# The mixer of a two-layer block, reordered: projection units, convolution taps and recurrence interleaved, some taps computed by ScalarE and GpSimd, norms applied after the matmuls

## The chip, the cores and the metric

The kernel runs on one core of a Trainium2 chip. The metric is the device time of one launch in microseconds. TensorE (PE) multiplies matrices, VectorE (DVE), ScalarE (ACT) and GpSimd (POOL) work elementwise, and SyncE (SP) issues the weight loads.

## The reference, cut to what matters

512 tokens of width 1024 pass a block of a mixer and a retrieval feed-forward (`peer_ffn`), then two attention layers with feed-forwards. The change concerns the mixer and what is next to it:

```python
def hybrid_mixer(n, w_in, ...):                     # n = rms_norm(h, mix_norm_g)
    z = n @ w_in                                     # 1024 -> 2048
    x_lru, g_lru, a_glu, b_glu = split(z, 4)         # 512 channels each
    xc = depthwise_conv(x_lru, lru_conv_w, ...)      # 4 taps
    h_fwd, h_bwd = rg_lru(xc, ...), rg_lru(xc, ..., reverse=True)
    y_lru = (h_fwd + h_bwd) * gelu(g_lru)
    glu = a_glu * sigmoid(b_glu)
    c = depthwise_conv(glu, conf_conv_w, ...)        # 31 taps
    y_conv = silu(group_layer_norm(c))               # groups of 64 channels
    y = concat([rms_norm(y_lru, beta_lru), rms_norm(y_conv, beta_conv)])
    return y @ w_out                                 # then h = h + this

# rg_lru: a = exp(log_a), log_a = 8 * sigmoid(gate r) * log_sigmoid(lam)
#         u = sqrt(-expm1(2 * log_a)) * sigmoid(gate i) * xc, scanned along the tokens
# peer_ffn(rms_norm(h, ffn_norm_g)): queries, top 16 keys of each head, 16384-row tables
# gathered by index, softmax gates, a weighted sum of rows
```

## The kernel before

Every tensor of the mixer lies with 128 channels on the partitions and the 512 tokens along the free axis, so 512 channels are four tiles, called c = 0 to 3. The code is a queue of instructions for each engine, written out by hand, with semaphores between them. There is no planner: the order in each queue is the order of the text.

**Projection.** `w_in` comes in 16 units of 512 KB (eight 128x128 blocks each) through a ring of four buffers, which SP fills (L1562). `stream` (L384) runs eight matmuls for a unit into one of four PSUM banks and waits until the bank's former tile was drained (`tile_drained`). The units come in the order `pairs`: first the four pairs of a_glu and b_glu, then the four of x_lru, then the four of g_lru. Before the first unit the whole norm stands: ScalarE squares the eight tiles of x (L363), TensorE sums them with a matrix of ones (L372), ScalarE takes the root (L367), VectorE its reciprocal (L377) and eight scaled tiles (L380). At the start PE also forms the rows of position biases (L1586), which later attention layers use; ScalarE copies them (L1635) and stores them to DRAM.

**Convolution.** VectorE multiplies a_glu and sigmoid(b_glu) out of PSUM (L1753) and then does all 31 taps of tiles 0 and 1, and later of tiles 2 and 3, in `scalar_tensor_tensor` instructions of 128x512 with the accumulator as second input (L1757, L1762). The 4 taps on x_lru follow (L1773, L1778).

**Gates and recurrence.** TensorE forms four gates for each tile (L1601), ScalarE their sigmoids (L1665), then eight Tanh (L1672) and eight Exp (L1677). VectorE turns the tanh into 1 - a*a by a division over 128x2048 elements, twice (L1793 to L1798, the reciprocal is L1796), ScalarE takes the root (L1681), and VectorE scans both directions (L1806).

**Norms of the mixer and output.** Group means and variances come from matmuls with a block matrix (L1608, L1612); VectorE takes four reciprocals (L1814) and products (L1816), ScalarE the SiLU (L1693). Both halves are then normalised in full (L363 to L380 again, once for each) before `stream` starts the eight units of `w_out`. VectorE adds each tile to the residual h (L544), ScalarE squares it, and the norm of the feed-forward again stands as a whole before the first query matmul (L596).

**Retrieval.** `peer_pe`, `peer_act`, `peer_dve` and `peer_pool` run 256 groups of two rows: GpSimd gathers them (L888), VectorE takes dot products (L827), ScalarE a GELU (L726), VectorE makes two diagonal matrices (L838), TensorE adds the weighted rows (L639). The first lookup begins with the copy at L753. Buffers return to GpSimd through `uv_used`.

`Steps.do` counts VectorE's own instructions, and `settle` waits for all of them. An instruction that reads what the one before wrote waits in this way.

## Time and profile before

| | |
|---|---|
| median of 3 runs | 3395.56 us (3392.03 to 3396.84) |
| the profiled execution | 3395.28 us, its span 3393.5 us |
| mixer and norms, to the first query matmul | 0 to 372.0 us |
| first lookup on VectorE | 390.84 us |
| gathers and their sums | to 1761.6 us |
| attention layers and feed-forwards | 1761.6 to 3393.5 us |
| mean granted TensorE clock | 0.964 of full |

The span is the part of the execution that the trace covers, and the execution's own time is 1.8 us longer. Times in rows are microseconds from the start of the span unless marked ns. A row of a timeline gives the start, the duration, engine, line, operation, what it writes and reads, and the count if several equal ones were merged; in square brackets is the idle time before it and what ended it. In a row of the chain the work is only the part that set the end.

### The profile page before, as it was taken

Reading aid. Unit: us, or ns where it says so; the run is one execution under the profiler, and the core shown is the slowest. Engines: PE = TensorE matmul, PEld = TensorE weight load, DVE = VectorE, ACT = ScalarE, POOL = GpSimd, SP = SyncE. Lnnn points to the kernel's source line nnn. Section 1 sums busy time; section 2 is a strip of 40 time slices with the busy share of each in tenths; the row PEclk is TensorE's granted clock in tenths of the full one; section 3 lists DMA queues with packets and bytes.
Section 4 is the critical chain, followed back from the end, with each engine's and each line's share of the span. In section 5 each row is a group of like instructions: output and inputs, shape, how many; then the busy total and the mean of one; then the engine's idle time right before and its main releaser. Section 6 shows DMA issues by size and latency. Waiting matters only on the chain.

```text
span 3393.5 us, 33892 instructions
## 1 busy us (share of the span) xinstructions
PE 2881.5 (85%) x11216; PEld 1744.1 (51%) x11216; DVE 1953.8 (58%) x5012; ACT 786.5 (23%) x1550; POOL 1141.6 (34%) x804
## 2 busy tenths in 40 slices
PE   6846888977777777777779998999999989999998
PEld 2312434423332222232238865688788867568876
DVE  2964366678888888888763486444212147344411
ACT  2041111111111111111121286222132147422211
POOL 0000023354444444444433232244444433134442
PEclk9877999999999999999999999999999999999999
DMA  3101389999999999999972111222222222122221
GB/s 95 58 17 43 136 306 353 345 410 427 427 427 427 426 427 427 426 417 425 419 289 75 51 51 49 79 95 93 95 85 93 92 75 80 34 82 97 94 94 67
DMA packets 121784, 696.21 MB, mean 205 GB/s; under 512 B 15003, under 2 KB 19243, under 8 KB 55435
## 3 DMA queue, kind: packets, MB, share of 16 engines
q0 software_dynamic: 74352, 543.06, 38.8%
q1 hardware_dynamic: 47184, 150.88, 13.8%
q10 hardware_dynamic: 124, 0.75, 0.1%
q8 instruction: 62, 1.02, 0.1%
q14 instruction: 62, 0.51, 0.0%
HBM read 692.30 MB, written 2.34 MB: 205 GB/s over the span
## 4 chain that ended last, share of the span: by engine, by line
PE 58%; DMA 23%; DVE 8%; issue 4%; ACT 3%; POOL 2%; DVEq 0%; SPq 0%; ACTq 0%; POOLq 0%
PE ps L520 30%; DMA arena<-in_peer_uv,arena 16%; PE ps L397 8%; PE ps L639 7%; DMA n<-in_peer_uv,arena 4%; DMA ring<-in_peer_uv,arena 3%; PE ps L596 3%; PE ps L1086 2%; PE ps L1102 2%; PE ps L1073 2%; POOL arena L888 2%; DVE arena L827 1%; ACT arena L1124 1%; PE ps L372 1%; PE ps L1347 1%
## 5 line engine op out<-in xcount | busy, mean ns | idle before, releaser
L639 PE MATMUL ps<-arena 128*128 128x512 f32 x1560 | 741.8, 621 | 215.0 <-DVE arena L838 214.7
L417 POOL TENSOR_TENSOR w_lo<-ring,w_hi 128x1024 fp32r<-128x1024 f32 (+1 forms) x176 | 459.2, 2609 | 745.9 <-ACT w_hi L430 745.9
L888 POOL DMA_INDIRECT arena<-in_peer_uv,arena x390 | 419.9, 1077 | 715.9 <-PE ps L639 544.0
L639 PEld LDWEIGHTS ps<-arena 128*128 128x128 f32 x1560 | 292.4, 196 | 655.2 <-DVE arena L838 342.2
L827 DVE CUSTOM_DVE_ANT_0 arena<-arena,sq 128x1024 f32<-128x1024 f32 x390 | 462.7, 1224 | 215.2 <-DMA arena<-in_peer_uv,arena 213.8
L520 PE MATMUL ps<-n_hi,w_hi 128*128 128x512 f32 x1152 | 461.7, 401 | 6.2 <-ACT n_hi L457 5.8
L520 PE MATMUL ps<-n_lo,w_hi 128*128 128x512 f32 x1152 | 455.9, 400 | 4.2 <-DVE n_lo L462 4.0
L520 PE MATMUL ps<-n_hi,w_lo 128*128 128x512 f32 x1152 | 457.1, 397 | 0.0
L430 ACT CAST w_hi<-ring 128x1024 fp32r<-128x1024 f32 (+1 forms) x176 | 194.8, 1107 | 770.9 <-PE ps L520 769.7
L726 ACT ACTIVATE arena<-arena 128x2 f32<-128x2 f32 x256 | 52.1, 203 | 1134.6 <-DVE arena L827 1134.6
L520 PEld LDWEIGHTS ps<-n_lo,w_hi 128*128 128x128 f32 x1152 | 219.0, 190 | 61.5 <-DVE n_lo L462 9.3
L520 PEld LDWEIGHTS ps<-n_hi,w_hi 128*128 128x128 f32 x1152 | 219.2, 190 | 60.0 <-issue 9.0
L544 DVE TENSOR_TENSOR h<-ps,h 128x512 f32<-128x512 f32 x40 | 27.7, 692 | 383.8 <-PE ps L520 222.5
L520 PEld LDWEIGHTS ps<-n_hi,w_lo 128*128 128x128 f32 x1152 | 218.6, 190 | 52.1 <-issue 0.5
L397 PE MATMUL ps<-n,ring 128*128 128x512 f32 x384 | 172.6, 613 | 33.8 <-DVE n L380 18.1
L838 DVE TENSOR_SCALAR arena<-consts,arena,tcmp 128x128 f32<-128x128 f32 x512 | 153.5, 342 | 0.0
L945 DVE TENSOR_TENSOR arena<-ps,rstd 128x512 f32<-128x512 f32 x44 | 30.5, 692 | 207.2 <-PE ps L520 207.2
L520 PE MATMUL ps<-hid_hi,w_hi 128*128 128x512 f32 x352 | 138.7, 394 | 12.4 <-DVE hid_lo L954 12.4
L639 PE MATMUL ps<-ring,arena 128*128 128x512 f32 x240 | 112.7, 613 | 38.6 <-DVE arena L838 38.6
L639 PE MATMUL ps<-n,arena 128*128 128x512 f32 x248 | 114.3, 603 | 34.9 <-DVE arena L838 34.9
L397 PEld LDWEIGHTS ps<-n,ring 128*128 128x128 f32 x384 | 75.5, 198 | 131.0 <-issue 120.6
L520 PE MATMUL ps<-hid_lo,w_hi 128*128 128x512 f32 x352 | 138.4, 393 | 0.0
(245 smaller groups left out, 3904.9 us busy)
## 6 DMA issues: line engine op xcount, KB each, us to landing
ring<-in_a_up SPq DMA_DIRECT2D x44, 512.0 KB, 3.7
ring<-in_b_up SPq DMA_DIRECT2D x44, 512.0 KB, 3.7
ring<-in_b_q SPq DMA_DIRECT2D x24, 512.0 KB, 3.7
ring<-in_a_down SPq DMA_DIRECT2D x16, 704.0 KB, 4.0
ring<-in_b_down SPq DMA_DIRECT2D x16, 704.0 KB, 4.0
ring<-in_a_in SPq DMA_DIRECT2D x20, 512.0 KB, 3.7
ring<-in_w_in SPq DMA_DIRECT2D x16, 512.0 KB, 3.7
ring<-in_w_q SPq DMA_DIRECT2D x16, 512.0 KB, 5.7
```

The source lines that it names most:

```text
L397: mm = pe.matmul(bank(j), ring[:, j, k * P:(k + 1) * P], rhs[k], start=k == 0, stop=k == kt - 1)
L417: pool.tensor_tensor(w_lo[:, j % 2, 0:kt * P], ring[:, j, 0:kt * P], w_hi[:, j % 2, 0:kt * P], ALU.subtract).then_inc(split_lo, 1)
L430: act.copy(w_hi[:, j % 2, 0:kt * P], ring[:, j, 0:kt * P]).then_inc(split_hi, 1)
L520: mm = pe.matmul(bank(j // 2 if two else j), w[:, j % 2, cols], r[:, x, :], start=no == 0 and not (two and j % 2), stop=no == len(passes) ...
L596: mm = pe.matmul(bank(2 + x), ring[:, u % RING, k * P:(k + 1) * P], ns[k], start=k == 0, stop=k == DK - 1)
L639: mm = pe.matmul(bank(2 * (tt % 2) + q), diag[:, no % DIAGS, r, :], uvrow[p][r][:, D + 512 * q:D + 512 * q + 512], start=slot + r == 0, st ...
L827: ins = dve.tensor_tensor_reduce(out=u, in0=u, in1=ntok[:, tt, :], scale=1.0, scalar=0.0, op0=ALU.mult, op1=ALU.add, accum_out=dots[:, p, ...
L838: ins = dve.tensor_scalar(diag[:, no % DIAGS, r, :], ident, gel[:, p, r:r + 1], gate[:, tt, slot + r:slot + r + 1], ALU.mult, ALU.mult)
L888: pool.indirect_dma_start(uvrow[p][r], None, t["peer_uv"], bass.IndirectOffsetOnAxis(ap=expert_id[:, tt, slot + r:slot + r + 1], axis=0)). ...
L1073: pe.matmul(b.scores, b.q, b.keys, start=True, stop=True).then_inc(L.scores_ready, 1)
L1086: tr = pe.transpose(ps[0:width, 4 + no % 2, P * x:P * x + P], L.p[:, s % 3, at:at + width], ident)
L1102: mm = pe.matmul(ps[64 * half:64 * half + 64, out_bank(L, it), P * qt:P * qt + P], v, L.pt[0:width, s % 2, P * x:P * x + P], start=y == 0, ...
```

## The change

The parts, in the order of the launch:

1. **Loads.** x comes in four pieces with a semaphore each, the first unit of w_in after the first piece; vec is loaded by ScalarE's queue; the constants come after the second unit. The one-hot table and the bias rows leave the start: SP loads the table in two halves when all lookups are done, TensorE forms one row chunk behind each of eight late groups (`BIAS_AT`), ScalarE copies it and stores the rows in two DMAs.
2. **Norm of the mixer late.** ns is x times the gain only (a `tensor_scalar`). TensorE starts on unit 0 as pieces of x arrive; the squares are added on VectorE and one matmul sums them. Each drained unit is multiplied by rstd (`drain`, VectorE, from PSUM). Before, ScalarE or the GLU product read the bank itself.
3. **Order.** Units go b_glu, a_glu for tiles 0 and 1, then x_lru, then tiles 2 and 3, then g_lru. PE's queue puts group means, variances and gates between units, VectorE's queue puts drains and norms between taps.
4. **Taps split.** Of 31 taps of a tile, the first 15, 15, 12 and 8 (`POOL_TAPS`) are products on ScalarE into four buffers (`PRODS`), added by GpSimd in two alternating sums. VectorE does the other 16, 16, 19 and 23 into two partial sums, adds them, and adds GpSimd's sum (`conv_merge`).
5. **Recurrence.** 1 - a*a comes from a square and one `scalar_tensor_tensor` (`lru_weight`); the two 2048-wide reciprocals with their `tensor_scalar` are gone. GpSimd multiplies igate and xc (128x2048, twice).
6. **Group norm.** A matrix I - mean centres a tile in one matmul; the four subtractions on VectorE are gone.
7. **Norms of the output late.** w_out multiplies y_conv * beta_conv and y_lru * beta_lru * ratio, where ratio is the quotient of both norms' factors. The factor of y_conv is applied to each finished tile before the residual. Units 0 to 3 take their convolution half first.
8. **Norm of the feed-forward late.** Queries and dot products use h times the gain; the factor for each token is given to Exp and Gelu as their scale (`tok_scale`).

The queues of the mixer after, cut to the order and the new functions:

```diff
+POOL_TAPS = (15, 15, 12, 8)
+PRODS = 4
...
+        LOOKUPS_DONE = ALL_GROUPS - 2 * GROUPS
+        BIAS_AT = [ALL_GROUPS - x for x in (13, 12, 11, 10, 7, 6, 5, 4)]
...
+                act.activation(ex, ex, ACT.Exp, scale=tok_scale[:, tt:tt + 1]).then_inc(ex_done, 1)
...
@@ sync
+                    sp.wait_ge(ids_ready, TT * PH)
+                    sp.dma_start(relb[0:NBUCKET, :], t["rel_bias_2"]).then_inc(rel_in, 16)
+                    for x in range(2):
+                        if x:
+                            sp.wait_ge(row_ready, 4)
...
+                    load_x(0)
+                    load(0, 0, True)
+                    for k in range(1, TT):
+                        load_x(k)
+                    load(0, 1, True)
+                    sp.dma_start(consts[:, :], t["consts"]).then_inc(const_in, 16)
+                    load(0, 2, True)
+                    load(0, 3, True)
@@ tensor
-            norm_mean(pe, "mix", ones_d)
-            pe.wait_ge(n_ready, norm_tiles["mix"] + DK)
-            stream(pe, "w_in", ns)
...
+            project(0)
+            pe.wait_ge(const_in, 16)
+            pe.wait_ge(row_added, DK - 1)
+            pe.matmul(bank(4), ones_d, sq[:, 0, :], start=True, stop=True).then_inc(mean_done, 1)
+            for u in range(1, 7):
+                project(u)
+            pe.wait_ge(root_done, MEANS["mix"])
+            center_group(0)
+            project(7)
+            group_variance(0)
+            project(8)
+            center_group(1)
+            project(9)
+            group_variance(1)
+            project(10)
+            project(11)
+            lru_gates()
+            center_group(2)
+            project(12)
+            group_variance(2)
+            center_group(3)
+            project(13)
+            group_variance(3)
+            project(14)
+            project(15)
...
+            for j in range(RING):
+                out_unit(j, range(LK, DK))
...
+            for j in range(RING):
+                out_unit(j, range(LK))
+            for j in range(RING, DK):
+                out_unit(j, [*range(LK, DK), *range(LK)])
@@ scalar
+            def products(c, taps):
+                act.wait_ge(glu_ready, c + 1)
+                for tap in taps:
+                    x = first_prod[c] + tap
+                    if x >= PRODS:
+                        act.wait_ge(pool_added, prod_used[x - PRODS])
+                    act.activation(prods[:, x % PRODS, :], gpad[:, c, tap:tap + T], ACT.Copy,
+                                   scale=col("conf_w", LK * tap + c)).then_inc(prod_ready, 1)
...
+            sigmoid(0)
+            products(0, range(9))
+            sigmoid(1)
+            products(0, range(9, POOL_TAPS[0]))
+            products(1, range(10))
+            center_square(0)
+            products(1, range(10, POOL_TAPS[1]))
+            group_root(0)
+            sigmoid(2)
+            conv_out(0)
+            center_square(1)
+            group_root(1)
+            products(2, range(6))
+            sigmoid(3)
+            products(2, range(6, 9))
+            keep_gates(0)
+            products(2, range(9, 11))
+            keep_gates(1)
+            products(2, range(11, POOL_TAPS[2]))
+            products(3, range(2))
+            keep_gates(2)
+            products(3, range(2, 4))
+            keep_gates(3)
+            products(3, range(4, POOL_TAPS[3]))
...
@@ vector
+            def conv_taps(c, between={}):
...
+                    if i >= 2:
+                        dve.wait_ge(dve_step, marks[i - 2])
+                        step.do(dve.scalar_tensor_tensor(out=x, in0=src, scalar=w, in1=x, op0=ALU.mult, op1=ALU.add))
...
+            conv_taps(0)
+            drain(2, sigb[:, 1, :])
+            drain(3, glu_in(1))
+            glu(1, 3)
+            conv_taps(1, {8: lambda: drain_x(0)})
+            conv_merge(0)
+            lru_conv(0)
+            for c in range(1, LK):
+                drain_x(c)
+                lru_conv(c)
+            conv_merge(1)
+            normalize(0)
+            drain(8, sigb[:, 2, :])
+            drain(9, glu_in(2))
+            glu(2, 9)
+            conv_taps(2, {3: lambda: normalize(1), 10: lambda: drain(10, sigb[:, 3, :])})
+            drain(11, glu_in(3))
+            glu(3, 11)
+            conv_taps(3, {8: lambda: conv_merge(2)})
+            conv_merge(3)
+            drain(12, gelug[:, 0, :])
+            lru_weight(0)
+            lru_weight(1)
+            drain(13, gelug[:, 1, :])
+            normalize(2)
+            lru_scan(0)
+            normalize(3)
+            drain(14, gelug[:, 2, :])
+            lru_scan(1)
+            drain(15, gelug[:, 3, :])
...
@@ gpsimd
+            for c in range(LK):
+                conv_adds(c)
+            pool.wait_ge(gates_read, 4 * LK)
+            for d in range(2):
+                pool.tensor_tensor(igate[:, d], igate[:, d], xc, ALU.mult).then_inc(ix_ready, 1)
```

`conv_adds` is `POOL_TAPS[c] - 1` instructions `tensor_tensor` of 128x512 with both inputs in SBUF: 14, 14, 11 and 7. `normalize` is a reciprocal (128x512) and a product; `lru_scan` a product (128x2048) and four scans; `lru_conv` one `tensor_scalar` and three dependent `scalar_tensor_tensor`; `conv_out` on ScalarE a SiLU, a square and a copy. ScalarE's queue goes on with the eight Tanh, `center_square(2)`, four Exp and a square for each direction, `center_square(3)`, the roots, three GELUs, `conv_out` of tiles 1 to 3 and the last GELU, then the root of the convolution's norm and the squares of y_lru.

## Rows read from the trace of the kernel before

**Rows 1.** The page: the span, and busy time of each engine.

```profile
span 3393.5 us, 33892 instructions
...
PE 2881.5 (85%) x11216; PEld 1744.1 (51%) x11216; DVE 1953.8 (58%) x5012; ACT 786.5 (23%) x1550; POOL 1141.6 (34%) x804
```

**Rows 2.** The chain that ended last, 0 to 400 us: start us, us, what.

```profile
1.19 15.12 DMA h<-in_x
...
123.46 58.01 PE ps L397 x128
...
208.40 12.97 DVE arena L1796
...
297.60 57.98 PE ps L397 x128
...
372.04 15.43 PE ps L596 x32
```

**Rows 3.** Busy time of each engine in the mixer's recurrence.

```profile
186.00:300.00 114.00, 30.49 (x57) 12.37 (x56) 86.11 (x42) 40.63 (x56) 0.55 (x1) 0.65 0.01 2
```

**Rows 4.** First microseconds: the last two columns are DMA share and GB/s.

```profile
4.00:8.00 4.00, 0.00 (x0) 0.00 (x0) 0.00 (x0) 0.00 (x0) 1.93 (x3) 1.00 0.96 292
...
12.00:16.00 4.00, 0.07 (x1) 0.00 (x0) 0.00 (x0) 0.00 (x0) 0.00 (x0) 1.00 0.99 185
```

**Rows 5.** Timeline of VectorE in the mixer, then the first lookup.

```profile
124.88 39.87 DVE L1762 SCALAR_TENSOR_TENSOR arena<-arena,vec 128x512 f32<-128x512 f32 x60
...
244.57 4.57 DVE L1806 TENSOR_TENSOR_SCAN arena<-arena 128x512 f32<-128x512 f32 x4
...
260.50 3.35 DVE L1814 RECIPROCAL arena<-sq 128x512 f32<-128x512 f32 x1
263.88 0.69 DVE L1816 TENSOR_TENSOR arena<-arena 128x512 f32<-128x512 f32 x1
...
355.62 0.69 DVE L544 TENSOR_TENSOR h<-ps,h 128x512 f32<-128x512 f32 x1 [6.17 <-PE ps L397]
...
390.84 0.29 DVE L753 COPY arena<-arena 128x256 f32<-128x256 f32 x1 [18.85 <-ACT arena L709]
```

**Rows 6.** Timeline of ScalarE in the mixer.

```profile
201.06 1.28 ACT L1677 ACT_TABLE_LOAD   x1
202.35 5.01 ACT L1677 ACTIVATE arena<-arena 128x512 f32<-128x512 f32 x8
...
244.18 2.17 ACT L1687 ACTIVATE sq<-arena 128x512 f32<-128x512 f32 x4
```

**Rows 7.** Timeline of TensorE: eight instructions, then eight like them.

```profile
278.05 6.01 PE L372 MATMUL ps<-sq,consts 128*128 128x512 f32 x8 [27.60 <-ACT sq L363]
285.35 3.70 PE L372 MATMUL ps<-sq,consts 128*128 128x512 f32 x8 [1.30 <-ACT sq L363]
```

**Rows 8.** GpSimd's groups by shape, whole span: count, busy, mean ns.

```profile
L417 POOL TENSOR_TENSOR w_lo<-ring,w_hi 128x1024 fp32r<-128x1024 f32 x144 | 355.8, 2471 | 598.9 <-ACT w_hi L430 598.9
L417 POOL TENSOR_TENSOR w_lo<-ring,w_hi 128x1408 fp32r<-128x1408 f32 x32 | 103.3, 3229 | 147.0 <-ACT w_hi L430 147.0
...
L1257 POOL TENSOR_SCALAR arena<-arena 128x512 f32<-128x512 f32 x8 | 15.9, 1992 | 46.8 <-DVE arena L1167 46.8
```

**Rows 9.** Timeline of GpSimd, 1766 to 1775 us.

```profile
1766.73 2.35 POOL L417 TENSOR_TENSOR w_lo<-ring,w_hi 128x1024 fp32r<-128x1024 f32 x1 [1.64 <-ACT w_hi L430]
1771.96 2.56 POOL L417 TENSOR_TENSOR w_lo<-ring,w_hi 128x1024 fp32r<-128x1024 f32 x1 [2.87 <-ACT w_hi L430]
```

**Rows 10.** Timeline of VectorE at the same time.

```profile
1767.30 2.33 DVE L462 SCALAR_TENSOR_TENSOR n_lo<-h,in_gain,n_hi 128x512 fp32r<-128x512 f32 x1 [2.17 <-ACT n_hi L457]
...
1772.21 2.86 DVE L462 SCALAR_TENSOR_TENSOR n_lo<-h,in_gain,n_hi 128x512 fp32r<-128x512 f32 x1
```

**Rows 11.** Busy time of each engine in the gather stage.

```profile
1000.00:1400.00 400.00, 301.82 (x651) 118.20 (x650) 331.01 (x974) 45.05 (x112) 172.91 (x161) 0.99 1.01 427
```

**Rows 12.** The chain late in the gather stage.

```profile
1730.53 20.89 DMA n<-in_peer_uv,arena
```

More of the change, by code:

```diff
@@ L284, in program @@
         assert max(a.at, a2.at) <= ARENA - 4 * 11 * P
+        assert after <= 14000
+        relb = Region(14000).take(NH)
+        tail = Region(28 * T)
+        onehot, rowbuf = tail.take(HALF_ROWS), tail.take(HALF_ROWS)
         tabA = Region(ARENA - 4 * 11 * P).take(2, 2, 896)
@@ L621, in turn_tokens, with token_means @@
                     tr.then_inc(tok_turned, 1)
+            def token_means():
+                pe.wait_ge(row_added, 2 * DK - 2)
+                for tt in range(TT):
+                    mm = pe.matmul(ps[:, 1, tt:tt + 1], sq[:, 0, P * tt:P * tt + P], ones_d[:, 0:1], start=True, stop=True)
+                mm.then_inc(mean_done, 1)
             for hd in range(HEADS_FIRST):
@@ L1613, in _, with project @@
-            pe.wait_ge(cstd_ready, LK)
-            norm_mean(pe, "conv", ones_l)
-            norm_mean(pe, "lru", ones_l)
-            pe.wait_ge(n_ready, norm_tiles["lru"] + LK)
-            stream(pe, "w_out", ns)
+            def project(u):
+                if u >= RING:
+                    wait_tile(pe, u)
+                pe.wait_ge(w_landed[u % RING], 16 * (u // RING + 1))
+                for k in range(DK):
+                    if u == 0:
+                        pe.wait_ge(mix_ready, k + 1)
+                    mm = pe.matmul(bank(u % RING), ring[:, u % RING, k * P:(k + 1) * P], ns[k], start=k == 0, stop=k == DK - 1)
+                mm.then_inc(unit_done, 1)
@@ L1658, in _ @@
-            for c in range(LK):
+            act.dma_start(vec[:, :], t["vec"]).then_inc(vec_in, 16)
+            for k in range(DK):
+                act.wait_ge(x_in[k // 2], 16)
+                act.activation(sq[:, k, :], hs[k], ACT.Square).then_inc(row_squared, 1)
+            act.wait_ge(lam_dve, 1)
+            act.activation(lamw[:, 1, :], lamw[:, 0, :], ACT.Exp, scale=-1.0).then_inc(lam_act, 1)
+            act.wait_ge(const_in, 16)
+            act.wait_ge(mean_done, MEANS["mix"])
+            act.activation(std[:, :], bank(4), ACT.Sqrt, bias=eps).then_inc(root_done, 1)
@@ new lines, in _ @@
+            for k in range(1, DK):
+                dve.wait_ge(row_squared, k + 1)
+                if k >= 2:
+                    dve.wait_ge(row_added, k - 1)
+                dve.tensor_tensor(sq[:, 0, :], sq[:, 0, :], sq[:, k, :], ALU.add).then_inc(row_added, 1)
+            dve.wait_ge(lam_act, 1)
+            dve.tensor_scalar(lamw[:, 2, :], lamw[:, 1, :], 1.0, None, ALU.add).then_inc(lam_dve, 1)
+            dve.wait_ge(root_done, MEANS["mix"])
+            step.do(dve.reciprocal(rstd[:, :], std[:, :]))
@@ new lines, in conv_merge, with lru_conv @@
+            def conv_merge(c):
+                dve.wait_ge(pool_added, pool_ops[c + 1])
+                step.settle()
+                dve.tensor_tensor(cacc[:, c, :], cacc[:, c, :], parts[:, 2 * (c % 2), :], ALU.add).then_inc(conv_ready, 1)
+            def lru_conv(c):
+                dve.wait_ge(tile_drained, 4 + c + 1)
+                step.do(dve.tensor_scalar(xc[:, c, :], xpad[:, c, 0:T], col("lru_w", c), col("lru_b", c), ALU.mult, ALU.add))
+                for tap in range(1, LRU_TAPS):
+                    step.settle()
+                    ins = dve.scalar_tensor_tensor(out=xc[:, c, :], in0=xpad[:, c, tap:tap + T], scalar=col("lru_w", LK * tap + c),
+                                                   in1=xc[:, c, :], op0=ALU.mult, op1=ALU.add)
+                    if tap < LRU_TAPS - 1:
+                        step.do(ins)
+                    else:
+                        ins.then_inc(xc_ready, 1)
@@ new lines, in lru_scan @@
+            def lru_scan(d):
+                dve.wait_ge(root_ready, d + 1)
+                dve.wait_ge(ix_ready, d + 1)
+                step.do(dve.tensor_tensor(igate[:, d], igate[:, d], wrk[:, d], ALU.mult))
+                step.settle()
+                for c in range(LK):
+                    order = slice(None, None, -1) if d else slice(None)
+                    step.do(dve.tensor_tensor_scan(tanh_la[:, d, c, order], rgate[:, d, c, order],
+                                                   igate[:, d, c, order], 0.0, ALU.mult, ALU.add))
@@ L1800, in _ @@
[L1800 to L1807 removed]
+                                     op0=ALU.mult, op1=ALU.add).then_inc(lam_dve, 1)
```

482 lines of the change are left out of this document (286 added, 196 removed).

## The prediction, made before the changed kernel had run

> **What bounds the kernel now.** I read the page first: TensorE is busy for 85% of the span and VectorE for 58% [rows 1], but these are means over stages, and the change touches only what stands before the first query matmul at 372.04 us. So the chain comes next [rows 2]. It runs through the arrival of x (to 16.31 us), the projection (58 us for eight units behind the first convolution), the recurrence with VectorE's reciprocals of 12.97 us, then 57.98 us for w_out, and only then the queries. No two of these overlap on the chain. The windows confirm it: from 186 to 300 us VectorE is busy 86 of 114 us, TensorE 30, at 0.65 of its clock, and the DMA share is 0.01 [rows 3]. Behind the mixer stands the gather stage, whose DMA share is 1.01 at 427 GB/s [rows 11]; its bytes don't change, so a lookup that starts earlier should carry the whole rest of the launch along. The end to watch is therefore the first lookup at 390.84 us [rows 5].
>
> **Unit costs.** VectorE: a tap 39.87 / 60 = 0.665 us, a drain or product 0.69, a dependent one 0.72, a reciprocal 3.35, a scan 4.57 / 4 = 1.14 [rows 5]. ScalarE: 2.17 / 4 = 0.54 for a product, 1.28 for a table switch [rows 6]. TensorE: the tiles of w_out are 6.17 + 0.69 = 6.86 us apart [rows 5], and eight matmul instructions after an idle stretch took 6.01 us where the next eight took 3.70 [rows 7]: a cold start costs about 1.8 us for a unit.
>
> **The unknown: GpSimd's adds beside VectorE's taps.** Before, GpSimd does no 128x512 add. Its 128x1408 subtraction takes 3.229 us and its fastest 128x1024 one 2.35 [rows 8, 9]; the line through them gives 1.18 us for 512 columns, the line through the means (2.471) gives 1.46. I take 1.3. Below stands 1.18; above, its `tensor_scalar` of 128x512 at 1.99 [rows 8]. What an add does to VectorE is seen where both ran. GpSimd worked from 1766.73 to 1769.08; VectorE's instruction of 1767.30 took 2.33 us, to 1769.63, which is 0.55 after GpSimd's end. GpSimd worked from 1771.96 to 1774.52; the one of 1772.21 took 2.86, to 1775.07, again 0.55 behind [rows 9, 10]. Both have two inputs in SBUF, and so do taps and adds. VectorE doesn't slow down, it stands still. The GpSimd instruction also took 2.56 instead of 2.35, so it had waited for the one on VectorE, and then got in ahead of the next. I therefore let the two alternate and charge VectorE 1.25 us for each add, 4.6 for each 128x2048 product (twice the 2.35 of 1024 columns, less the part that overlaps).
>
> The Trainium skill says the same and sharper (SBUF — State Buffer, Who interferes with whom): a VectorE instruction with two SBUF inputs and a GpSimd one that reads SBUF exclude each other for a whole instruction, so work given to GpSimd is not taken off VectorE. By that rule the 46 adds cost 46 x 1.25 = 57 us of VectorE's time to save 50 taps, 33 us; this case's trace agrees at the two places above.
>
> **The walk through the new order.** I follow VectorE's queue and stop it only where a semaphore does.
> - *Norm.* The early DMA rate is 185 to 292 GB/s [rows 4]. x, the first unit, vec and gw are about 3.3 MB where before x, the table and gw were 3.1, so x ends near 15.5 us (range 13 to 17). Two scalings 1.1, seven dependent adds 5.0: 21.6. One cold matmul 1.7, root 0.7, reciprocal 3.35: rstd at 27.4. The norm is no longer ahead of unit 0, but it is ahead of the first drain.
> - *Tile 0.* Unit 1 ends at 23.3 + 6.9 + 1.8 = 32.0; drain, GLU and the small lambda operations: 35.1. Sixteen taps and a sum 17 x 0.665 = 11.3, fourteen adds 17.5: 63.9.
> - *Tile 1.* Two drains and GLU 2.1: 66.0. 11.3 + 0.7 + eight adds 10.0: 88.0. Only eight, since ScalarE's queue holds products 10 to 14 behind `center_square(0)`, which needs `conv_merge(0)`, which stands behind these taps. PE stands at `center_group(0)` from about 71 us too, so units 7 and later are late. Merge: 88.7.
> - *Four `lru_conv`* at 0.5 + 3 x 0.72 = 2.7: 10.8, three drains 2.1, the six adds left 7.5, `conv_merge(1)` 0.7: 109.8.
> - PE now gets `center_group(1)` 0.9 and unit 9, 6.9: 117.6; drain and GLU: 119.0.
> - *Tile 2.* Three taps, then a wait for group 1's deviation to about 122.4, `normalize` 4.1, the other seventeen instructions 11.3, a drain 0.7, five adds that hit them 6.3: 144.8. Drain and GLU: 146.2.
> - *Tile 3.* Twenty-five instructions 16.6, eleven adds (four of tile 2 are left) 13.8, both 2048-wide products 9.2: `conv_merge(3)` at 185.8.
> - *Recurrence.* PE can only now do `center_group(3)` and unit 13, cold: 9.5, to 195.3, and `drain(13)` waits for it in front of everything else. The two `lru_weight` (4.6) hide in that wait. Then drain 0.7, `normalize` 4.1, scan 2.3 + 4.6 = 6.9, `normalize` 4.1, drain 0.7, scan 6.9, drain 0.7: 219.4. Sums and products of four tiles 5.0: 224.4. The reciprocals of 2 x 12.97 us are gone.
> - *Output.* Square, add, matmul, root, reciprocal 3.35, ratio, first product: 7.9, to 232.3. PE meanwhile ends the convolution halves at 233.8. Four halves 13.7 and four units 27.5: 275.0, where before it was 355.6.
> - *Query.* The tiles of the last w_out unit need 2 us, covered by seven matmuls of the first query. Unit 0 ends at 281.9. Before, the lookup came 18.8 us after the query's start [rows 2, 5] with a cold start in it; now about 17.4. Lookup at 292.4.
>
> The gain is 390.8 - 292.4 = 98.4 us. Against it stand the table and the bias rows, 0.73 MB in a stage that moves 427 GB/s [rows 11]: 1.7 us. The matmul of a bias row fits: a group lasts 400 / (651 / 8) = 4.9 us, of which PE works 3.7 [rows 11], and one more costs 0.9. Sum: 3395.3 - 98.4 + 1.7 = 3298.6 against the profiled execution, 0.3 us from the median. I say 3299.
>
> ScalarE switches tables more often in the new order, four times on the stretch that ends at w_out, at 1.28 us by the row; the switch at 201.06 was followed at 202.35 by work [rows 6]. The Trainium skill (ScalarE: Activation LUTs, What ACT_TABLE_LOAD costs) counts 2.66 us with a drain for each; by it the time would be 5.5 us more, 3304, and the row speaks against it.
>
> **The rivals.**
> - *GpSimd and VectorE don't get in each other's way.* Then `conv_merge(3)` is set by PE's units and VectorE's own taps: 48.5 after tile 1's GLU, 78 after `conv_merge(1)` (unit 7), 90.8 at tile 2's GLU, 127.7 at the merge, 58 us earlier: 3241. Against it stand both stalls of [rows 9, 10]; for it, only that those were 1024 wide with a rounded output.
> - *An add is as long as the `tensor_scalar`*, 1.99 us [rows 8]: 0.74 more for 46 + 8 equivalents (a 2048-wide product is four): +40, 3339. For it, GpSimd's waits on semaphores between short adds; against it, the line through its own two-input shapes.
> - *The late table stalls the groups.* Its second half is asked for three groups (14.7 us) before its use; a transfer there took 20.89 us [rows 12]: 6.2 us for the wait, 3305. If all eight rows waited so, each for a copy behind a GELU, 50 us: 3349.
> - *Slower than before.* Gain and charge cross where an add holds VectorE for 1.25 + 96.7 / 54 = 3.0 us; then the taps alone eat the recurrence's saving. Only the 1408-wide instruction takes that long [rows 8], so this needs a handover of more than an add's own length each time.
>
> **The numbers.** Forecast (3285 to 3318 with its own uncertainties: x by 2 us, handovers of 0.05 to 0.2 us at 57 places, cold starts) 0.66; longer adds 0.15; no blocking 0.10; stalls at the late rows or another wait in the handwritten order 0.06; slower 0.03. The range 3250 to 3340 takes in the longer adds and most of the way to the free ones. 0.2% is 6.8 us, about what a measurement here can tell from no change: faster 0.96, same 0.01, slower 0.03.
>
> **What would show it.** In the changed profile: GpSimd's adds above 1.3 us each, near 1.8 where taps run; VectorE's taps alternating between 0.7 and 1.8 to 2.0; PE idle in front of the centring matmul from about 71 to 89 us and near 170 to 186; the lookup near 292; the gather stage as long as before. The prediction is wrong if taps keep 0.665 us beside adds, if `conv_merge(3)` is later than 200 us, or if the end of the gathers moves by less than the lookup.

## The result, and the profile after

Before: 3396.1 us (3392.03 to 3396.84, 4 runs). After: 3296.97 us (3292.27 to 3298.73, 4 runs). The ratio is 0.9708, 95% interval 0.9692 to 0.9725. The profiled execution took 3298.73 us. The forecast was 3299.0.

The page of the kernel after, span and busy times, as [rows 1]:

```profile
span 3296.9 us, 33551 instructions
...
PE 2856.2 (87%) x11182; PEld 1737.2 (53%) x11182; DVE 1960.2 (59%) x4995; ACT 858.7 (26%) x1614; POOL 1241.1 (38%) x855
```

The span is 96.6 us shorter, although VectorE is shown busy for 6 us more and GpSimd for 100 us more. Part of that busy time is one of them standing still for the other, as the experiments show. The gain comes from work laid side by side and from the reciprocals that are gone. The chain of waits, as [rows 2], shows where:

```profile
2.87 11.43 DMA h<-in_x
...
34.94 15.37 DVE arena L1942 x14
...
103.96 1.28 ACT L1801
105.25 0.82 ACT arena L1801
...
144.18 23.55 DVE arena L1942 x15
169.30 2.08 PE ps L1687 x2
171.37 8.13 PE ps L1680 x16
...
213.65 48.07 PE ps L1738 x112
...
268.58 0.79 PE ps L653 x8
```

Neither reciprocal of 12.97 us is left in it. Of the projection, which had a stretch of 58.01 us there, one unit is left (8.13 us). Of w_out's 57.98 us 48.07 are left (L1738): its 112 matmul instructions are seven units' worth, at sixteen a unit, so only one unit's worth was done early. VectorE's taps (L1942) are what the mixer now waits for until 169 us.

VectorE's timeline at the places that the walk named, as [rows 5]:

```profile
50.33 0.69 DVE L1949 TENSOR_TENSOR arena<-arena 128x512 f32<-128x512 f32 x1
...
168.55 0.69 DVE L1954 TENSOR_TENSOR arena<-arena 128x512 f32<-128x512 f32 x1
169.16 0.68 DVE L1922 TENSOR_TENSOR arena<-ps,rstd 128x512 f32<-128x512 f32 x1
169.76 4.48 DVE L1976 SCALAR_TENSOR_TENSOR arena<-arena 128x2048 f32<-128x2048 f32 x2
179.53 0.69 DVE L1922 TENSOR_TENSOR arena<-ps,rstd 128x512 f32<-128x512 f32 x1 [5.28 <-PE ps L1680]
...
279.72 0.29 DVE L830 COPY arena<-arena 128x256 f32<-128x256 f32 x1 [9.85 <-ACT arena L767]
```

The first lookup moved from 390.84 to 279.72 us, by 111.1, where I had expected 98.4. The total moved by less. So the first thing to see is that something gave 12.7 us more than forecast and something later took it back. Three lines of three views say where. They are 400 us of the gather stage, beginning 609 us after the first lookup as those of [rows 11] do (the last column is GB/s), SyncE's timeline where it starts the weights of the next layer, and the groups of TensorE's matmuls for the bias rows:

```profile
889.00:1289.00 400.00, 297.22 (x641) 116.29 (x640) 326.60 (x961) 53.03 (x111) 170.56 (x158) 0.99 1.01 421
```

```profile
1671.19 116.93 SPq L1650 DMA_DIRECT2D ring<-in_a_in  x20
```

```profile
L696 PE MATMUL ps<-arena x16: 345/589/600, 1610.0 to 1657.6; 33*16 33x512 f32 x14, 33*16 33x219 f32 x2
```

That first load waits for the last gathered row to be used, so it marks the end of the gather stage. Before, it stood at:

```profile
1761.86 39.87 SPq L1562 DMA_DIRECT2D ring<-in_a_in  x8
```

From the first lookup to it are 1371.0 us before and 1391.5 after. The DMA share is 1.01 in both, but 421 GB/s flow where 427 did. The rest of the span is 1631.6 us before and 1625.7 after. Together: -111.1 + 20.4 - 5.9 = -96.6. I had put 1.7 us where 20.4 stand.

The experiments use the same three pieces. I call them the mixer (to the first lookup), the gather stage (to the first `a_in` load) and the later layers (to the end of the span).

### The profile page after: what moved, and what is told of

Its sections match the earlier page's. It is cut to its first block, busy times and chain, and to the rows that moved or that the text cites. A ratio compares the mean times of both kernels' runs of the same rounds, so it can differ in the third digit from the quotient of the medians.

```text
span 3296.9 us, 33551 instructions
## 1 busy us (share of the span) xinstructions
PE 2856.2 (87%) x11182; PEld 1737.2 (53%) x11182; DVE 1960.2 (59%) x4995; ACT 858.7 (26%) x1614; POOL 1241.1 (38%) x855
## 4 chain that ended last, share of the span: by engine, by line
PE 54%; DMA 25%; DVE 10%; issue 4%; ACT 3%; POOL 2%; SPq 0%; DVEq 0%; ACTq 0%; POOLq 0%
PE ps L535 31%; DMA arena<-in_peer_uv,arena 16%; PE ps L674 7%; DMA ring<-in_peer_uv,arena 5%; DMA n<-in_peer_uv,arena 4%; PE ps L412 3%; PE ps L623 3%; DVE arena L1942 3%; PE ps L1166 2%; PE ps L1182 2%; PE ps L1153 2%; PE ps L1738 1%; POOL arena L968 1%; DVE arena L904 1%; ACT arena L1204 1%
## 5 line engine op out<-in xcount | busy, mean ns | idle before, releaser
L432 POOL TENSOR_TENSOR w_lo<-ring,w_hi 128x1024 fp32r<-128x1024 f32 (+1 forms) x176 | 465.9, 2647 | 733.8 <-ACT w_hi L445 733.8
L787 ACT ACTIVATE arena<-arena,tok_scale 128x2 f32<-128x2 f32 x256 | 75.5, 295 | 1093.1 <-DVE arena L904 1092.3
L535 PE MATMUL ps<-hid_hi,w_lo 128*128 128x512 f32 x352 | 138.6, 394 | 0.0
L1166 PE MATMUL ps<-consts,arena 128*128 128x128 f32 (+1 forms) x800 | 114.6, 282 | 23.5 <-ACT arena L1204 18.4
```

The costliest lines, as they stand in the source:

```text
L432: pool.tensor_tensor(w_lo[:, j % 2, 0:kt * P], ring[:, j, 0:kt * P], w_hi[:, j % 2, 0:kt * P], ALU.subtract).then_inc(split_lo, 1)
L535: mm = pe.matmul(bank(j // 2 if two else j), w[:, j % 2, cols], r[:, x, :], start=no == 0 and not (two and j % 2), stop=no == len(passes) ...
L787: act.activation(gel[:, p, :], dots[:, p, :], ACT.Gelu_apprx_tanh, scale=tok_scale[:, tt:tt + 1]).then_inc(gel_ready, 1)
L1166: tr = pe.transpose(ps[0:width, 4 + no % 2, P * x:P * x + P], L.p[:, s % 3, at:at + width], ident)
```

## The experiments

Two questions were open: what takes the 20 us in the gather stage, and whether GpSimd's adds cost or save. Nothing of the gathers is in the diff. But `center` adds 128 columns to `consts`, and `tok_std` and `tok_scale` are new. These stand ahead of the arena in SBUF. Added up from the allocations, the arena begins at byte 99840 before, a multiple of 256, and at 100416 after, 64 bytes past one. `n`, `sq` and the ring begin 128 bytes past a multiple of 256 in both kernels. Gathered rows of 8 KB land in the arena, `n` and the ring.

**A gap of 192 bytes ahead of the arena.**

```diff
+        sb("gap", [P, 48])
         arena_at = nc.sbuf_base
```

> The changed kernel with 192 bytes of padding in front of the arena, so that the gather buffers in it begin at a multiple of 256 bytes again (100608), as they did before the change (99840), where the change had moved them to 100416. The new constants and token factors (576 bytes) had done that. In the changed kernel the saturated gather stage moves 421 GB/s instead of 427 and its median packet takes 312 ns instead of 309, so 350 MB of gathers take 11.7 us more and the whole stage 20 us more. If the start address is the cause: 427 GB/s and 309 ns again, 12 to 16 us faster than the changed kernel, about 3283 us. Rival, the rate differs from chip to chip or run to run, or the longer ScalarE instructions with a scale set it: 421 GB/s here too and 3297 us.

Measured: 3287.3 us (3285.01 to 3288.99), ratio 0.9678 [0.9665, 0.9692]. The gather stage at its old rate, and its end:

```profile
889.00:1289.00 400.00, 301.83 (x650) 118.31 (x650) 330.87 (x976) 53.34 (x112) 168.39 (x161) 0.99 1.01 427
```

```profile
1655.80 118.28 SPq L1651 DMA_DIRECT2D ring<-in_a_in  x20
```

Mixer 278.7, gather stage 1377.1 (14.4 shorter), later layers 1631.0 (5.3 longer, as before the change). The rate is back at 427 GB/s, as the theory had it, but the total fell by 9.7 us and not by 12 to 16, because the later layers gave 5.3 back. The address of the arena sets the rate of the gathers. That it also sets something in the later layers I had not expected.

A stage as a whole is a coarse measure: in the kernel after and in the four kernels below that share its addresses it takes 1386.7 to 1391.5 us. Counted in the trace's packets of 8 KB, the stretch from the 24,000th to the 60,000th is finer. It takes 693.7 to 696.0 us in the five kernels of this document with the arena on a multiple of 256, and 704.6 to 707.0 in the six with it 64 bytes past.

**A second gap, so that n, sq and the ring begin at multiples of 256 bytes too.**

```diff
+        sb("gap0", [P, 32])
         h = sb("h", [P, DK, T])
...
+        sb("gap", [P, 16])
         arena_at = nc.sbuf_base
```

> As the one before, and 128 bytes of padding in front of h as well, so that the two gather buffers in n and the two in the weight ring, which start 128 bytes off a multiple of 256 in every kernel so far, are aligned too. If a start off the boundary costs about 1.4 to 2% of a packet: 2 of 7 buffer pairs gain it, 0.5% of 1170 us, another 4 to 7 us, about 3278 us, and more than 427 GB/s. Rival: no difference to the run before.

Measured: 3268.27 us (3265.55 to 3271.28), ratio 0.9624 [0.9611, 0.9637].

```profile
889.00:1289.00 400.00, 302.39 (x652) 118.36 (x650) 331.84 (x975) 53.33 (x112) 171.20 (x161) 0.99 1.01 427
```

The rate stays at 427 GB/s, where I had expected more: for a transfer, a start 128 bytes past costs nothing that shows here. The gather stage is 4.6 us shorter, but this is no gain of the rate: the whole of it lies ahead of the 16,000th packet, where kernels with the same addresses differ by as much (399.4 to 404.2 us from the first lookup to there in the five with the arena of the kernel after). The total is 19.0 us lower, and most of that came in the later layers, 1612.5 us in place of 1631.0, where TensorE is the bound.

**The kernel before, with its arena 64 bytes later.**

```diff
+        sb("gap", [P, 16])
         arena_at = nc.sbuf_base
```

> The kernel before with 64 bytes of padding in front of the arena and nothing else, so its gather buffers lose their 256-byte alignment (99904). If the start address is the cause: 421 GB/s in the saturated stage, packets of 312 ns, and 12 to 16 us slower than the kernel before, about 3410 us. Rival: 427 GB/s and 3396 us.

Measured: 3398.47 us (3394.94 to 3402.53), ratio 1.0007 [0.9998, 1.0016]. The total did not move, against the expectation. The pieces did:

```profile
1000.00:1400.00 400.00, 298.40 (x640) 116.95 (x639) 327.04 (x962) 44.83 (x111) 171.31 (x159) 0.98 1.01 421
```

```profile
1777.05 16.31 SPq L1563 DMA_DIRECT2D ring<-in_a_in  x5
```

Gather stage 1385.6 us (14.6 longer, as expected), later layers 1621.9 (9.7 shorter). Two effects of one address cancel. A total alone would have cleared the address of all blame.

**The kernel before, with n, sq, ring and arena all at multiples of 256 bytes.** This takes the second effect alone.

```diff
+        sb("gap0", [P, 32])
         h = sb("h", [P, DK, T])
...
+        sb("gap", [P, 32])
         arena_at = nc.sbuf_base
```

> The kernel before with two gaps in SBUF and nothing else: 128 bytes ahead of the first tensor, so that n, sq and the weight ring start at multiples of 256 bytes, and 128 bytes ahead of the arena, which stays at such a multiple. Theory (TensorE's products run a little faster when both operands start so: 232.1 to 227.3 ns per split matmul was seen between the kernels of the first batch): gather stage unchanged at 1371 us (+-3), the layers behind it 1610 to 1618 us in place of 1631.6, total 3374 to 3383. Rival (the shorter later layers of the all-aligned kernel came from elsewhere, or the arena's own place is what counts): total within 4 us of 3396.

Measured: 3376.18 us (3374.5 to 3376.95), ratio 0.9942 [0.9928, 0.9955]. Gather stage 1369.6, later layers 1613.0, all three as the theory had them. So two gaps and no other edit give 0.6%. Windows of 220 us, beginning about 420 us after the first `a_in` load (417 in the third), show it in TensorE's count. The first column behind the width is its busy time with the number of matmuls; the lines are of the kernel before, the kernel after, and this one:

```profile
2181.90:2401.90 220.00, 220.00 (x948) 178.35 (x947) 101.45 (x98) 51.72 (x60) 100.13 (x40) 1.00 0.31 97
```

```profile
2091.20:2311.20 220.00, 220.00 (x963) 180.51 (x962) 104.29 (x100) 52.88 (x60) 100.72 (x41) 1.00 0.29 98
```

```profile
2179.10:2399.10 220.00, 220.00 (x972) 182.23 (x971) 103.32 (x100) 53.06 (x60) 100.79 (x41) 1.00 0.30 100
```

TensorE is busy without a gap in all three, at the full granted clock, with 948, 963 and 972 matmuls: 232.1, 228.5 and 226.3 ns for one.

The same is seen over a whole up-projection of a feed-forward, by how long SyncE takes to issue its 44 weight loads, since each waits for a buffer that TensorE has used. The lines are of the first feed-forward before, of both in the kernel after, and of the first in this one:

```profile
2136.74 251.05 SPq L1562 DMA_DIRECT2D ring<-in_a_up  x44
```

```profile
2043.68 248.33 SPq L1650 DMA_DIRECT2D ring<-in_a_up  x44
...
2870.82 251.95 SPq L1650 DMA_DIRECT2D ring<-in_b_up  x44
```

```profile
2134.02 245.19 SPq L1564 DMA_DIRECT2D ring<-in_a_up  x44
```

In all kernels of this document it is 250.9 to 252.1 us with the arena on a multiple and the rest 128 bytes past (four stretches) and 245.2 to 246.3 with all on multiples (six). With the arena 64 bytes past it is 247.4 to 248.4 in ten stretches and 252.0 and 252.6 in two, the second one of the kernel after and the first one of the kernel with the old recurrence weight. So this address doesn't fix the pace alone, and why two stretches fell back isn't known. The trace also narrows down which products it concerns. In the up-projection one operand lies in `n` or `sq` (`n_hi`, `n_lo`) and the other in the arena (`w_hi`, `w_lo`). In the down-projection both lie in the arena (`hid_hi`, `hid_lo`), and SyncE's 16 loads for it take 114.4 to 116.3 us in all kernels, with no order by address.

**All taps on VectorE.** ScalarE's products and GpSimd's adds go, and `conv_merge` with them.

```diff
-POOL_TAPS = (15, 15, 12, 8)
+POOL_TAPS = (0, 0, 0, 0)
...
-            conv_taps(3, {8: lambda: conv_merge(2)})
-            conv_merge(3)
+            conv_taps(3)
...
-            for c in range(LK):
-                conv_adds(c)
```

> The changed kernel with the split of the taps undone: all 31 taps of a tile on VectorE in two partial sums, summed at once, no products on ScalarE and no adds on GpSimd; the order of the units and everything else stay. If VectorE stands still while GpSimd adds: VectorE's own 50 extra taps cost 50 x 0.665 = 33 us and the 46 adds, at about 1.0 us of standstill each in the changed kernel's trace, give back 46, and the centring of tiles 0 and 1 no longer waits for a late merge. The last centring then comes near 158 us instead of 169, the lookup about 11 us earlier, 3286 us. Rival, the split takes work off VectorE as it was meant to: the last centring comes 20 to 33 us later, 3317 to 3330 us.

Measured: 3281.25 us (3275.84 to 3281.59), ratio 0.9654 [0.9641, 0.9667], so faster than the kernel after. VectorE does 50 taps more and comes to the first lookup 11.6 us earlier, where the first theory had 11 and its rival had it come later. Its timeline with GpSimd idle (the first line) and beside GpSimd's two products of 2048 columns (the second), GpSimd's line, and the lookup:

```profile
33.99 19.30 DVE L1926 SCALAR_TENSOR_TENSOR arena<-arena,vec 128x512 f32<-128x512 f32 x29
...
129.39 27.86 DVE L1926 SCALAR_TENSOR_TENSOR arena<-arena,vec 128x512 f32<-128x512 f32 x29
...
268.15 0.29 DVE L827 COPY arena<-arena 128x256 f32<-128x256 f32 x1 [9.84 <-ACT arena L764]
```

```profile
131.50 9.96 POOL L2074 TENSOR_TENSOR arena<-arena 128x2048 f32<-128x2048 f32 x2 [125.46 <-ACT arena L1809]
```

The same 29 instructions take 8.56 us more beside GpSimd, nearly all of GpSimd's 9.96.

**The adds alone left out.** The products stay on ScalarE, the 74 taps on VectorE.

```diff
-                        act.wait_ge(pool_added, prod_used[x - PRODS])
+                        act.wait_ge(prod_ready, x - PRODS + 1)
...
-            for c in range(LK):
-                conv_adds(c)
```

> The kernel after, with GpSimd's 50 accumulating instructions left out: ScalarE still computes its 50 tap products and VectorE its 74 taps, but the products are never added, so the convolution misses those taps (and VectorE's sum is taken twice where the merge stood). Theory (GpSimd's adds hold up VectorE's taps): the taps fall to the 0.665 us each that the kernel with all taps on VectorE showed (29 in 19.30 us), so that 50 taps fewer than there take 50 x 0.665 = 33 us off its end of the taps (158.0), plus 4 merges of 0.7: the last merge ends at about 128 us, at most 135 if projection units are then late (169.2 in the kernel after); the first lookup comes at 240 to 248 us and the total is 3255 to 3272. Rival (the taps take as long without the adds, and something else spaces them): last merge at about 169, total within 5 us of the kernel after.

Measured: 3259.21 us (3254.07 to 3262.49), ratio 0.9597 [0.9584, 0.961]; first lookup at 243.71, last merge ending at 134.0. The first theory holds in all three. VectorE's first tile, against 15.44 us for the same 14 in the kernel after, and its last merge:

```profile
34.19 9.36 DVE L1942 SCALAR_TENSOR_TENSOR arena<-arena,vec 128x512 f32<-128x512 f32 x14
...
114.08 10.02 DVE L1942 SCALAR_TENSOR_TENSOR arena<-arena,vec 128x512 f32<-128x512 f32 x15
124.13 4.90 DVE L1949 TENSOR_TENSOR arena<-arena 128x512 f32<-128x512 f32 x1
129.06 4.90 DVE L1953 TENSOR_TENSOR arena<-arena 128x512 f32<-128x512 f32 x1
```

```profile
118.18 15.23 POOL L2097 TENSOR_TENSOR arena<-arena 128x2048 f32<-128x2048 f32 x2 [112.36 <-ACT arena L1812]
```

Two additions of 512 columns, 0.69 us elsewhere, took 4.90 each: one product of 2048 columns on GpSimd for each. And the lock works both ways. GpSimd's first product is shown from 118.18 on, yet the nine of the fifteen taps that were left went through at their own 0.67 us until 124.1. Its two took 15.23 us here, 9.96 above. Why it had to wait longer here than there stays open.

**The old recurrence weight in the new order.** Per direction a `tensor_scalar`, a reciprocal of 2048 columns and a product, in place of ScalarE's square and one product.

```diff
-                dve.scalar_tensor_tensor(out=wrk[:, d], in0=wrk[:, d], scalar=1.0, in1=tanh_la[:, d],
-                                         op0=ALU.add, op1=ALU.mult).then_inc(w_ready, 1)
+                step.do(dve.tensor_scalar(wrk[:, d], tanh_la[:, d], -1.0, 1.0, ALU.mult, ALU.add))
+                step.do(dve.reciprocal(wrk[:, d], wrk[:, d]))
+                dve.scalar_tensor_tensor(out=wrk[:, d], in0=tanh_la[:, d], scalar=-2.0, in1=wrk[:, d],
+                                         op0=ALU.mult, op1=ALU.mult).then_inc(w_ready, 1)
```

> The kernel after, with the recurrence's input weight computed the old way: per direction one VectorE tensor_scalar, the 2048-wide reciprocal and the product, in place of ScalarE's square and one product. From the rows before, per direction 1.22 + 12.95 us more on VectorE. Theory (both reciprocals lay on the path): from 169.8 us on, two times 16.5 us until 202.8, where the kernel after starts the drain of unit 13 at 179.5 because it waits 5.3 us for TensorE there: +23.3 us at that point, first lookup at 303, total 3315 to 3325. Rival (ScalarE and GpSimd are what the part waits for, the reciprocals fit into their waits): first lookup within 5 us of 279.7, total below 3303.

Measured: 3318.43 us (3311.81 to 3321.51), ratio 0.9772 [0.9758, 0.9785]; first lookup at 304.39. From 171.33 us on:

```profile
172.58 12.95 DVE L1972 RECIPROCAL arena<-arena 128x2048 f32<-128x2048 f32 x1
...
189.03 12.95 DVE L1972 RECIPROCAL arena<-arena 128x2048 f32<-128x2048 f32 x1
202.01 2.29 DVE L1974 SCALAR_TENSOR_TENSOR arena<-arena 128x2048 f32<-128x2048 f32 x1
204.22 0.68 DVE L1916 TENSOR_TENSOR arena<-ps,rstd 128x512 f32<-128x512 f32 x1
```

The drain of unit 13 comes 24.7 us later than in the kernel after and no longer waits, and the lookup is later by the same 24.7. These are the 28.4 us by which VectorE's instructions are longer, less the 5.3 us of wait for unit 13 that they fill, and 1.6 us by which the last merge had already ended later. The first theory holds, and the cheaper formula is worth 21.5 us in the median time, a good fifth of the whole gain.

**The bias rows in the mixer.** The table is loaded behind the first four weight units, and the eight matmuls stand behind projection unit 6, where TensorE would idle for 15.7 us.

```diff
                     load(0, 3, True)
+                    sp.dma_start(onehot[0:NBUCKET + 1, :], t["onehot"]).then_inc(onehot_in, 16)
+                    sp.dma_start(relb[0:NBUCKET, :], t["rel_bias_2"]).then_inc(rel_in, 16)
...
-                if no in BIAS_AT:
-                    bias_row(BIAS_AT.index(no))
```

> The kernel after, with the bias rows computed in the mixer again: table loaded behind the first four weight units, 8 TensorE products after projection unit 6, 8 ScalarE copies after the tenth product of tap tile 1, one store. Nothing of them is left in the gather stage, neither the table's transfer nor the 8 products in the last 13 groups. Theory (the late rows take about 6 of the 20 us that the gather stage lost): from the first lookup to the end of the gathers 1385.5 us against 1391.5, the mixer up to 1 us longer, total 3290 to 3294. Rival (the lost time is the transfers' slower pace alone): stage and total within 2 us of the kernel after. Second rival: the table's 0.5 MB among the first weight units holds the projection up by its 2.6 us and more, total unchanged.

Measured: 3287.24 us (3284.35 to 3288.38), ratio 0.9678 [0.9665, 0.9691]. First lookup at 279.09, next weights at:

```profile
1667.03 116.59 SPq L1609 DMA_DIRECT2D ring<-in_a_in  x20
```

The gather stage is 1387.9 us, 3.5 shorter, where 6 had been expected. By itself that is within the spread: with the late rows and the same addresses the kernel with the old recurrence weight needed 1386.7. The end of the stage decides it. From the 60,000th packet to the first `a_in` load the four kernels with late rows and these addresses take 126.2 to 127.3 us, and the two without (this one and the kernel before with its arena shifted) 123.5 and 123.3. So the rows cost about 3 to 4 us. The mixer doesn't take longer for it (both theories of a cost there fall), since TensorE and ScalarE had room before `center_group(0)`. The total gained 9.7 us, more than this explains. In the profiled executions 6.2 lie in the later layers, which the edit does not touch. 4.2 of those are in the second feed-forward. From its first weights to the load of the next matrix the kernel after needs 257.2 us in its profile, while three kernels with the same addresses as it (this one and the two above) need 252.8 to 253.0. This is the slow second up-projection of the kernel after (251.95 us). The kernel with the old recurrence weight has such a one in its first feed-forward (252.59). I count 3.5 us as shown and the rest as variation between executions.

**Together.** All taps on VectorE, all starts at multiples of 256 bytes, the rows early, and three edits in the order:

```diff
-            conv_taps(2, {3: lambda: normalize(1), 10: lambda: drain(10, sigb[:, 3, :])})
+            conv_taps(2, {18: lambda: normalize(1), 10: lambda: drain(10, sigb[:, 3, :])})
...
-                pool.tensor_tensor(igate[:, d], igate[:, d], xc, ALU.mult).then_inc(ix_ready, 1)
+                dve.tensor_tensor(igate[:, d], igate[:, d], xc, ALU.mult).then_inc(ix_ready, 1)
...
-            center_group(2)
-            project(12)
+            project(12)
+            project(13)
+            center_group(2)
```

> The version that the experiments point to: all 31 taps of each tile on VectorE, SBUF starts of n, sq, ring and arena at multiples of 256 bytes, bias rows computed in the mixer, normalize(1) after the 18th tap of tile 2 in place of the third, projection units 12 and 13 ahead of the third centring on TensorE, and the two 2048-wide products of the recurrence's input on VectorE in place of GpSimd. Sum from the runs: 3281.3 (all taps on VectorE), less 28.7 (all aligned, 3297.0 to 3268.3), less 3.5 to 5 for the rows, less 4.5 and 5.0 us of VectorE's waits for the second group root and for unit 13, less 3.7 (two products of 2.28 us on VectorE in place of the 8.3 us by which GpSimd's held VectorE up): about 3235, within 3225 to 3245; first lookup at about 255. Rival (the gains overlap: where VectorE no longer stands, it waits for TensorE's units or for ScalarE's squares): first lookup at 262 or later, total 3246 to 3256.

Measured: 3248.32 us (3244.8 to 3250.61), ratio 0.9565 [0.9552, 0.9578], the fastest of all. But my sum of 3235 missed, and the rival's range holds it. First lookup and end of the gathers:

```profile
108.82 0.69 DVE L1888 TENSOR_TENSOR arena<-ps,rstd 128x512 f32<-128x512 f32 x1 [2.69 <-PE ps L1640]
...
129.50 0.55 DVE L1912 TENSOR_SCALAR arena<-arena,vec 128x512 f32<-128x512 f32 x1
129.97 0.48 DVE L1910 TENSOR_SCALAR arena<-arena,vec 128x512 f32<-128x512 f32 x1
130.36 19.29 DVE L1908 SCALAR_TENSOR_TENSOR arena<-arena,vec 128x512 f32<-128x512 f32 x29
...
260.73 0.29 DVE L797 COPY arena<-arena 128x256 f32<-128x256 f32 x1 [9.84 <-ACT arena L749]
```

```profile
1631.27 116.30 SPq L1608 DMA_DIRECT2D ring<-in_a_in  x20
```

The last tile's 29 taps are back at 19.29 us. The mixer gave 7.4 of 13 us, because waits for projection units (2.39 us for unit 9 and 2.69 for unit 10) stand where group 1's deviation was waited for. In the later layers I had counted part twice: the profile with all taps on VectorE had 1620.9 us already, against 1625.7 for the kernel after with its slow stretch. The gather stage is 1370.5 us, 1371.0 before the change, so the two causes, addresses and rows, leave nothing of the 20.4 us open beyond the spread.

## Why the forecast was right, and where not

In the mixer the mechanism was right: most of the projection off the chain, 2 x 12.97 us of reciprocals gone, and VectorE held up by GpSimd's adds so that the saving of the split is eaten. What was wrong is that the whole rest of the launch is carried along unchanged. One of my own signs of being wrong came true: the end of the gathers moved by 90.7 us, less than the lookup's 111.1, and the gather stage was not as long as before. Against the walk the mixer came 12.7 us early, the gather stage 18.7 late and the later layers 5.9 early. That these cancel, and the total came within 2 us, is luck.

- *Norm and first GLU.* x ended at 14.3 us for 15.5, rstd at 28.2 for 27.4. Right.
- *"Sixteen taps and a sum, fourteen adds 17.5: 63.9."* Measured 51.0. This count was wrong: seven adds ran there, not fourteen. ScalarE's `sigmoid(1)` stands ahead of products 9 to 14 and waits for `drain(2)`, which stands behind these taps. GpSimd therefore had no work. Its idle time stands in brackets:

```profile
36.04 8.41 POOL L2110 TENSOR_TENSOR arena<-arena 128x512 f32<-128x512 f32 x5
53.04 7.45 POOL L2110 TENSOR_TENSOR arena<-arena 128x512 f32<-128x512 f32 x5 [8.59 <-ACT arena L1788]
```

  The adds left over ran beside tile 1, which took 29.0 us to its merge for 24.8 in the walk. The walk had used this very argument for tile 1 and `center_square(0)`, and missed it for tile 0.
- *"1.25 us for each add."* The period beside taps is 8.41 / 5 = 1.68 us and holds one tap of 0.665, so VectorE loses 1.0. Tile 1 says the same: 29.0 less 14.1 of its own is 14.9 us for fifteen adds. I had let the add's whole length count; 0.25 us of it overlap with VectorE. Over some 46 adds that is 11.5 us, and 0.6 more for the two 2048-wide products (4.3 each, 4.6 assumed): 12.1 of the 16.6 us by which the last merge ended early, at 169.2 for 185.8. I have not taken the rest apart.
- *TensorE idle from about 71 to 89 us and near 170 to 186.* It was idle for 15.68 us to 80.1 and for 15.15 us to 169.3, with the taps as the releaser. The place was right; the times shifted with the taps.
- *"The two `lru_weight` hide in that wait."* They did, and 5.28 us of wait were left (the line of 179.53). The old formula fills this wait, so it costs less than the 28.4 us of its instructions.
- *Merge to first lookup.* Expected 106.6 us, measured 110.5, so 3.9 us were missing from the walk here; the lookup came 12.7 early, not 16.6. Of these 3.3 stand before the end of w_out. The walk had all four convolution halves done 48.0 us after the merge. In PE's queue the matmul of the second norm (L1749) stands behind the second of them and waits for the squares of y_lru until 212.5, 43.3 us after the merge, and the two halves left (6.9 us) come only then.
- *"A cold start costs about 1.8 us for a unit."* The two lines of [rows 7] give 6.01 - 3.70 = 2.3. After the wait that ended at 169.3, the centring took 2.08 us and unit 13 8.13, where they take 1.1 and 7.0 without one: 2.1 to 2.2 us in all.
- *"1.7 us for the table and the rows."* This is the step that failed. The sentence on which it rests, "its bytes don't change", says nothing about where they land. The stage lost 20.4 us: 14.4 by the arena's address (shown from both sides, 14.6 in the kernel before), 3 to 4 by the rows (shown by moving them). The rest, some 2 us, is less than the spread between kernels with the same addresses. The rival that had the rows stall the groups was there with 6.2 us. None had the address.
- *Table switches.* I had weighed 1.28 us a switch against 2.66 with a drain. In the chain after, the switch at 103.96 stands with 1.28 us and its work begins at 105.25, so the smaller price holds.
- *Later layers.* I forecast no change. They took 5.9 us less, in the same direction as the address effect on TensorE's interval (232.1 to 228.5 ns). Without the slow second up-projection it would have been about 10, as in the kernel before with its arena shifted (9.7).

The first rival, no blocking (3241), is refuted by both experiments on the taps; the longer adds (3339) by the period of 1.68 us. The Trainium skill's rule (SBUF — State Buffer, Who interferes with whom), that GpSimd and VectorE exclude each other on their shared port, is borne out: 4.90 us for an addition of 0.69. By it, work given to GpSimd is not taken off VectorE, and moving the 50 taps back gave 11.6 us.

## What to carry to other kernels

An address is an edit too: whatever is allocated ahead of a large buffer moves it, so pad buffers that receive gathered rows or feed TensorE, and compare stages, not totals, since one shift here cost 14.6 us in one stage and gave 9.7 back in another. Compare several kernels with the same addresses too, before a few microseconds of one stage are put down to an edit. Don't share element-wise work between VectorE and GpSimd where both read two tensors from SBUF; count it as done in turn, and expect the sharing to lose unless GpSimd's piece falls into a wait of VectorE. In a handwritten order, ask at every item of a queue what the item ahead of it waits for, for the engines that help as well as for the one on the path.

## What the hardware showed that I had not expected

- Gathers of 8 KB rows into an arena 64 bytes past a multiple of 256 ran at 421 GB/s, and at 427 with the arena on a multiple, with the same DMA share of 1.01. `n` and the ring, 128 bytes past, cost nothing more. The Trainium skill (DMA: Bandwidth & Descriptors, How a descriptor splits into AXI transactions) states that a transfer piece (descriptor) that does not start at a multiple of 256 bytes begins its first transaction at the boundary below. For 8 KB that would be 33 transactions in place of 32, an estimate of 3% from that page; the runs show 1.4%, and nothing for starts 128 bytes past, so the rule doesn't fit this case as it stands. The page words it for reads, and the side that was moved here is written.
- TensorE's interval depends on where its operands begin: 232.1 ns with the arena on a multiple and the rest 128 bytes past, mostly 228.5 with the arena 64 bytes past (232.8 in the one window of the kernel with the old recurrence weight), 226.3 to 226.6 with all on multiples, at a granted clock of 1.00. It shows where one operand lies in the arena and the other outside it, and not where both lie in the arena. Whether the distance between the two counts or each start by itself wasn't tried.
- The order in which VectorE and GpSimd get their turn isn't fixed: nine taps went past a waiting GpSimd product in one kernel, and in another (all taps on VectorE) the product shown from 131.50 got in after the tap then running.
